# Three hybrid transformer blocks on one core: two bank copies moved ahead of the square roots, one semaphore wait moved into the compression, and the merge put first in its slot of the attention

## The reference, cut to what matters

```python
x = x + 0.5 * swiglu_ffn(x, ffn1_norm[l], ffn1_w_gu[l], ffn1_w_down[l])
h = rms_norm(x, mix_norm[l])
x = x + hybrid_mixer(h, w_in[l], w_gate[l], ...)
x = x + 0.5 * swiglu_ffn(x, ffn2_norm[l], ffn2_w_gu[l], ffn2_w_down[l])
```

```python
o_a = stick_breaking_attention(sb_q, sb_k, sb_v)          # 4 heads
o_b = nsa_attention(nq, ...)   # 8 heads in 2 groups: compressed, selected and window keys
o_c = dsa_attention(dq, dk, dv, iq, ik, iw, ...)          # 4 heads, top 256 keys by an index score
g_a, g_b, g_c = jnp.split(jax.nn.sigmoid(h @ w_gate), 3, axis=-1)
merged = g_a * (o_a @ w_br_a) + g_b * (o_b @ w_br_b) + g_c * (o_c @ w_br_c)
return merged @ w_out
```

## Time and profile before

| what | us |
|---|---|
| three executions | 3588.35, 3590.3, 3590.64 |
| their median | 3590.3 |
| the profiled execution, its own time | 3588.37 |
| its span, first to last instruction | 3586.8 |
| PE busy in the span | 3507.7 (98%) |
| DVE busy in the span | 1930.0 (54%) |
| ACT busy in the span | 1460.2 (41%) |
| mean granted clock of PE | 0.993 of full speed |

### The profile page before, as it was taken

One profiled execution on the slowest core, in us unless ns is written; L12 is line 12 of the kernel. 1 busy time (PEld: TensorE's weight loads), 2 busy tenths in 40 slices (PEclk: granted clock), 3 DMA queues, 4 the chain that ended last, 5 costly groups with the idle time before them and its releaser, 6 DMA issues.

```text
span 3586.8 us, 46418 instructions
## 1 busy us (share of the span) xinstructions
PE 3507.7 (98%) x16692; PEld 2784.9 (78%) x16692; DVE 1930.0 (54%) x3221; ACT 1460.2 (41%) x2186; POOL 174.5 (5%) x181
## 2 busy tenths in 40 slices
PE   8999999999999999999999999999999999999998
PEld 6888876657888888888866577888887777878886
DVE  4443465767544344434647765543368776545433
ACT  4442345554444234423355544443233434534431
POOL 0000000000100000000000001000000001020001
PEclk9999999999999999999999999999999999999999
DMA  3223522114322322234221043222422222313231
GB/s 135 99 94 106 161 94 67 49 35 167 139 97 96 102 99 97 96 105 151 95 83 54 28 159 137 100 99 100 141 96 91 77 71 92 123 65 105 94 106 64
DMA packets 99831, 356.06 MB, mean 99 GB/s; under 512 B 11823, under 2 KB 12079, under 8 KB 98920
## 3 DMA queue, kind: packets, MB, share of 16 engines
q1 hardware_dynamic: 83232, 300.16, 25.0%
q10 hardware_dynamic: 9416, 30.34, 2.6%
q0 software_dynamic: 7040, 23.66, 1.8%
HBM read 330.98 MB, written 26.80 MB: 100 GB/s over the span
## 4 chain that ended last, share of the span: by engine, by line
PE 88%; DVE 7%; ACT 3%; issue 2%; DMA 0%; POOLq 0%; POOL 0%; ACTq 0%; DVEq 0%
PE bank L316 24%; PE bank L318 24%; PE bank L317 24%; PE bank L609 5%; PE bank L1041 1%; PE bank L1696 1%; DVE unit_lo L295 1%; PE bank L1070 1%; PE bank L1050 1%; PE bank L1669 1%; ACT unit_hi L290 1%; PE bank L1142 1%; PE bank L1685 1%; PE bank L1087 1%; PE bank L1132 1%
## 5 line engine op out<-in xcount | busy, mean ns | idle before, releaser
L295 DVE TENSOR_TENSOR unit_lo<-unit_raw,unit_hi 128x1024 fp32r<-128x1024 f32 x526 | 647.2, 1232 | 709.0 <-ACT unit_hi L290 698.7
L316 PE MATMUL bank<-h_hi,unit_hi 128*128 128x512 f32 x2416 | 955.8, 396 | 12.2 <-DVE unit_lo L295 7.1
L318 PE MATMUL bank<-h_hi,unit_lo 128*128 128x512 f32 x2416 | 942.5, 390 | 0.0
L317 PE MATMUL bank<-h_lo,unit_hi 128*128 128x512 f32 x2416 | 942.1, 390 | 0.0
L290 ACT ACTIVATE unit_hi<-unit_raw 128x1024 fp32r<-128x1024 f32 x526 | 552.6, 1052 | 354.9 <-PE bank L318 342.5
L316 PEld LDWEIGHTS bank<-h_hi,unit_hi 128*128 128x128 f32 x2416 | 454.7, 188 | 123.2 <-issue 21.5
L318 PEld LDWEIGHTS bank<-h_hi,unit_lo 128*128 128x128 f32 x2416 | 454.4, 188 | 96.2
L317 PEld LDWEIGHTS bank<-h_lo,unit_hi 128*128 128x128 f32 x2416 | 454.9, 188 | 92.2 <-issue 1.7
L316 PE MATMUL bank<-act_hi,unit_hi 128*128 128x512 f32 x880 | 346.7, 394 | 0.0
L318 PE MATMUL bank<-act_hi,unit_lo 128*128 128x512 f32 x880 | 345.0, 392 | 0.0
L317 PE MATMUL bank<-act_lo,unit_hi 128*128 128x512 f32 x880 | 341.5, 388 | 0.0
(11 more groups left out here) (305 smaller groups left out, 4515.3 us busy)
## 6 DMA issues: line engine op xcount, KB each, us to landing
unit_raw<-in_units SPq DMA_DIRECT2D x564, 512.0 KB, 3.3
gates_kept<-gate_z POOLq DMA_DIRECT2D x32, 256.0 KB, 2.3
sig_ab<-gates_kept ACTq DMA_DIRECT2D x16, 512.0 KB, 3.7
bias_rows<-bias_once POOLq DMA_DIRECT2D x2, 3840.0 KB, 19.0
x_kept<-x ACTq DMA_DIRECT2D x3, 2048.0 KB, 11.0
x<-x_kept ACTq DMA_DIRECT2D x3, 2048.0 KB, 8.3
xc<-xc ACTq DMA_DIRECT2D x16, 256.0 KB, 4.3
bias_t<-bias_rows POOLq DMA_DIRECT2D x16, 256.0 KB, 3.8
```

The lines of the kernel that those rows point to most:

```text
L295: nc.vector.tensor_tensor(w_lo[u % SLOTS][:], raw[u % SLOTS][:], w_hi[u % SLOTS][:].bitcast(F32), ALU.subtract).then_inc(unit_lo, 1)
L316: nc.tensor.matmul(out_ap, w_h, r_h, start=first, stop=False)
L317: nc.tensor.matmul(out_ap, w_h, r_l, start=False, stop=False)
L318: return nc.tensor.matmul(out_ap, w_l, r_h, start=False, stop=last)
```

## The change

Three edits.

In `mix1_act`, `out_t(1, 0)` and `out_t(1, 1)` (token blocks 0 and 1 of chunk 1) stand at the end of the splits of u = 15, ahead of the two roots of u = 15, and no longer at the start of u = 16.

In `mix1_pe` and `compress`, TensorE no longer waits for `t_out` at TB + 1 before unit 16. The wait stands in `compress`, before the first product of the compression, and the list `between` of unit 16 puts none of these products behind the first two of unit 16, and two behind the fifth and the eighth.

In `mix2_dve`, `merge_out` comes first in its slot, ahead of `reduce`, the splits of the gate units, the index sums and the weights.

```diff
--- before.py
+++ after.py
@@ -626,12 +626,10 @@
             c, j = divmod(u - 6, 4) if u < 16 else {16: (2, 2), 18: (2, 3), 20: (3, 0), 22: (3, 1), 24: (3, 2), 25: (3, 3)}[u]
             if u == 10:
                 pe.wait_ge(s["sb_out"], 4)
-            elif u == 16:
-                pe.wait_ge(s["t_out"], TB + 1)
             elif u == 20:
                 pe.wait_ge(s["t_out"], 2 * TB)
             read = {6: (s["x_val"], (1, 1, 2, 4)), 14: (s["t_out"], (1, 2, 3, 4)), 20: (s["zn"], (9, 9, 12, 12))}.get(u)
-            between = {16: one_each, 18: one_each, 20: [(), (), (), (), (0, 1), (2, 3), (4, 5), (6, 7)], 22: one_each}.get(u)
+            between = {16: [(), (), (0,), (1,), (2, 3), (4,), (5,), (6, 7)], 18: one_each, 20: [(), (), (), (), (0, 1), (2, 3), (4, 5), (6, 7)], 22: one_each}.get(u)
             natural_unit(pe, r, u, chunk_banks(c), 2 * j, 2, 512, j == 0, j == 3, read, s["block_made"] if j == 3 else None,
                          used=1 + len(MIX1_EMPTY) if u == 25 else 2 if between else 1, between=between)
             for cb in TURN_AFTER.get(u, ()):
@@ -658,6 +656,7 @@
         q = (u - 17) // 2
         if q == 0 and i == 0:
             pe.wait_ge(s["xc_in"], 16 * 8)
+            pe.wait_ge(s["t_out"], TB + 1)
         if i == 0:
             pe.wait_ge(unit_lo, SLOTS * r + u + 1)
         dst = bank[KV_BANKS[q // 2]][:, 0:G * NC].rearrange("p (g c) -> p g c", g=G)
@@ -692,13 +691,16 @@
                 a.then_inc(s["t_out"], 1)
 
             for c in range(3):
-                for b, at in enumerate(((12, 12, 13, 14), (12, 12, 13, 13), (15, 15, 17, 17))[c]):
-                    if u == at + 4 * c:
+                for b, at in enumerate(((12, 12, 13, 14), (None, None, 13, 13), (15, 15, 17, 17))[c]):
+                    if at is not None and u == at + 4 * c:
                         out_t(c, b)
             if u + AHEAD == MIX1_UNITS:
                 first_gate_hi(act, r)
             elif u + AHEAD not in MIX1_EMPTY and u + AHEAD < MIX1_UNITS + GATE_SLOTS:
                 split_hi(act, r, u + AHEAD)
+            if u == 15:
+                out_t(1, 0)
+                out_t(1, 1)
             if u in (1, 2, 3, 4):
                 q = u - 1
                 act.wait_ge(s["x_val"], q + 1)
@@ -1404,6 +1406,8 @@
         nc.vector.tensor_tensor(kc_lo[:], kc_t[:], kc_hi[:].bitcast(F32), ALU.subtract).then_inc(s["split_lo"], 1)
         for q in range(SLOT_END + 1):
             b, at = divmod(q, JOBS)
+            if merged(q):
+                merge_out(*merged(q))
             if q < SLOTS2:
                 reduce(q)
             if gate_split_at(q, 1):
@@ -1412,8 +1416,6 @@
                 index_sum(*bh)
             if weighted(q):
                 weigh(*weighted(q))
-            if merged(q):
-                merge_out(*merged(q))
             if b < TB and at == CMP_SHIFT:
                 compressed_shift(b)
             if b < TB and at == CMP_SCALE:
```

## The result

The changed kernel took 3564.27 us (median of 4 executions, 3564.03 to 3564.50) against 3589.32 before (4 executions, 3588.28 to 3590.64): 25.05 us less, ratio 0.993 with a 95% interval of 0.9913 to 0.9947. The forecast was 3566, with a range of 3561 to 3578. Of the later executions of the kernel before, one took 5309.46 us at a mean granted clock of 0.614 and is in no comparison here. The span of the profiled execution fell from 3586.8 to 3562.6 us, by 24.2, which is the sum of the prediction; the mean granted clock rose from 0.993 to 0.996.

What follows compares the result with a forecast made beforehand. TensorE was taken to set the end, so only filling its holes or restoring its clock pays. Projection 15.8 plus attention 8.4 makes 24.2 us, from the median 3590.3 to 3566.1, forecast as 3566, range 3561 to 3578.

Steps and rivals of the forecast that it cites:

- The cause of the projection's stall: Before unit 16: copies queue behind ScalarE's roots; moving them ahead removes TensorE's 4.26 us wait in both layers.
- The clock's term: Half clock behind removed stalls goes: 2.51 and 4.77 us in unit 16, 1.6 a layer behind slot 75.
- What is late next: After unit 16: VectorE's token block 3 and `unit_lo` of unit 19 arrive in time, with 0.4 us of cover.
- The merge: Attention, slot 75: merging first frees bank 5 early, removing waits of 2.65 and 2.7 us; 8.4 us with the clock.
- rival E: Attention: uncovered merges delay what is queued behind them, at most 13.8 us in both layers, giving 3579.9; chance 0.04.
- C: Slot 75: TensorE waits for something else of VectorE, not the bank; the 8.4 us go, 3574.5; chance 0.08.
- A: Projection and slot 75: stalls go but the half clock stays; only 13.9 us won, 3576.4; chance 0.09.
- B: Projection: stall moves to the turning of block 3 or unit 19; large form 3581.9, chance 0.06; 1 us a layer, 3568.
- D: Lines 1142 and 609: half clock falls behind shorter waits, 1.6 to 4.77 us an episode, up to 3613.8; chance 0.03.

Runs made afterwards that it cites:

- the copies alone: Kernel before with only the copies of token blocks 0 and 1 moved ahead of the roots; 3575.31 us, ratio 0.9953.
- the filled wait: Kernel before with TensorE turning token block 1 of chunk 1 eight times over, copies still behind the roots; 3581.35 us, ratio 0.9976.
- the last but one experiment: Changed kernel with the stick-breaking addition of slot 10 first in VectorE's slot in each query block; 3557.99 us, ratio 0.9915 to the kernel before.
- the merge alone: Kernel before with only `merge_out` moved first in its slot; 3581.62 us, ratio 0.998.
- the wait alone: Kernel before with only TensorE's wait moved into the compression and the products regrouped, copies behind the roots; 3586.21 us, ratio 0.9985.
- slot 75 alone: Changed kernel with the merge first in slot 75 only, late again in the eleven other slots; 3564.04 us.
- VectorE late: Changed kernel with two unused 128x512 additions on VectorE at u = 15, ahead of the squares of token blocks 2 and 3; 3566.27 us.
- without the second edit: Changed kernel with TensorE's wait back before unit 16 and the compression's products single, copies and merge still moved; 3564.60 us, on another chip.

## Why the prediction was right

**The cause of the projection's stall** was put in ScalarE's order, and the copies alone took it from 4.26 to 0.18 us. The wait's own move was costed at little, and is worth 0.4 us a layer.

**The clock's term** (2.51 + 4.77 + 1.6 + 1.6 = 10.5 of the 24.2 us) had the right cause in the projection, as the filled wait shows: 7.3 forecast, 8.0 measured. In slot 75 no wait was filled; what stands for the cause there is that the clock stays at 1.00 in the changed kernel, where the wait is gone. The sizes were right too: unit 16 went from 10.75 and 13.01 to 8.25 us. In all the projection gave a little more than forecast: 16.3 us came back there (7.0 in layer 0; in layer 1 the same distance went from 1765.59 - 1747.08 = 18.51 to 1745.84 - 1736.59 = 9.25, 9.3 less), against 15.8. The difference of 0.5 lies at the seam: the turning and unit 16 now overlap by 0.24 us in each layer (477.20 against 476.19 + 1.25 = 477.44), where I started unit 16 at the turning's end. It comes from the moved wait: without it unit 16 starts 1.42 us after the turning has begun (477.29 - 475.87), with it 1.01.

The prediction used the two costs of the same wait, 2.51 and 4.77 us, without a reason for the difference. The windows of the kernel before show one. In layer 0 the clock fell while TensorE still stood idle: it is at 0.50 from 481.00 to 481.55, and the stretch went on to about 487.0, so some of it passed in the wait. In layer 1 it is still at 1.00 from 1752.58 to 1753.30, behind the wait, and at 0.50 from 1753.38 to 1763.50, all of it in unit 16. Why it falls earlier in one layer than in the other isn't shown.

**What is late next** was read rightly. The forecast had 0.4 us of cover, and 1.2 us of delay (two additions at distances of 0.6) cost 0.83 us of waiting at the turning. The two waits are 1.7 us and the time rose by 2.0. From the start of this turning to unit 18 it is 487.92 - 486.01 = 1.91 us, where the changed kernel takes 486.29 - 485.45 = 0.84: 1.07 more, and 1.05 in layer 1. That is the wait and 0.2 us by which the two groups of four tiles no longer overlap.

**The merge**: one slot of twelve carries all of it (3564.04 with that slot alone). 4.1 us came back in each layer, where 4.2 were forecast. With the projection that is 16.3 + 8.2 = 24.5 us, and the span is 24.2 shorter; 0.15 of the difference is the kernel's first wait, 7.29 us instead of 7.14. The prediction had VectorE's slot no longer than before; it is a little longer, since the reduction behind the merge waits 0.27 us for ScalarE, and TensorE waits for nothing there. The reductions that stand behind the merge cost nothing, so rival E is out, and so is C.

**The rivals A and B** didn't come: unit 16 ran at 1.00, and the roots started 1.08 us after ScalarE had become free. D, the half clock behind shorter waits, didn't come in the changed kernel. Its list was incomplete: it had the waits on line 1142 and line 609, and not the four for `m_lo`, 6.7 us in all with 1.7 the longest. It is behind one of these that the half clock came in the last but one experiment, and it cost nothing there.

The forecast's 3566 is 1.7 us above the measured median, of which 1.0 is the median of before, forecast from at 3590.3 and 3589.32 with one execution more.

## What to carry to other kernels

On an engine that works through its list in order, an instruction that could run long ago may stand behind one whose input comes late; compare when its own input was ready with when it started, and move it ahead if it ends before the other's input comes. A stall of TensorE is to be priced with the half-clock stretch behind it, which in the kernel before cost 0.6 and 1.1 times as much again as the stall of 4.26 us. That price is due only if TensorE sets the time behind the stall; ahead of its next wait, as in the merge phase above, the slow stretch cost nothing. When such a stall can't be removed, harmless matmuls in it can bring back the clock's part; 28 turned tiles in a wait of 4.26 us did. And when an order of slots is shifted, look for the single slot in which the consumer stands in the same slot as the producer: that one was worth 8 us, the other eleven nothing that was measured. One more such place is left in the changed kernel: in the second block TensorE waits 4.11 us for `h_lo` (line 400) until 3167.86, and the clock is at 0.51 from there to 3174.20. No experiment tried to remove this wait.

## What the runs showed of the hardware

The cost of the half clock isn't a constant of the stall. The wait of 4.26 us cost unit 16 of layer 0 2.5 us in the profile of the kernel before; in that of the merge alone, which doesn't touch the projection, the window from 481.31 to 491.11 is 9.80 us at 0.83, 1.6 more than 8.24. The same wait of 2.65 us in slot 75 cost 1.7 us of clock in a profile of the kernel before, and 0.45 x 7.40 = 3.3 in layer 1 of the copies-alone kernel. It also goes with the scatter of the times. Each execution has its own mean granted clock, and the two run together: of the ten of the wait alone, the fastest (3578.49) has 0.995 and the two slowest (3589.88 and 3590.59) 0.991; of the four of the copies alone, 3570.06 has 0.996 and the others, 3575.07 to 3576.57, have 0.994. The kernels with waits of over 2 us left in the projection or slot 75 scattered by 6.5 us (the copies alone, 4 executions), 6.2 (the filled wait, 9), 8.8 (the merge alone, 10), 12.1 (the wait alone, 10) and 7.3 (the kernel before, 23). The four without them (the changed kernel, slot 75 alone, VectorE late, and without the second edit) scattered by 0.5 to 1.2 us in 4 each. The comparison is rough: the numbers of executions differ, the first four of the kernel before lay within 2.4 us, and all kernels keep the wait of 4.1 us in the second block.

Waits of 4.26, 2.65 and 2.29 us had a stretch at 0.50 behind them in each profile in which I looked, and those of 1.95 and 1.97 too; waits of 1.72, 1.21 and 0.83 us did not. The length of one wait doesn't settle it: in the second block of the kernel before, TensorE waits 0.66, then 1.65 us (until 3186.69), then 4.12, with a little work between, and the clock is at 0.51 from 3186.69 to 3197.20, so it fell ahead of the long wait. Turning tiles kept the clock up here: behind 36 of them in a row and the 1.21 us of waiting that were left, TensorE was at 1.00.
